# Index scores in pieces of 512 keys instead of 1024, with four places of scores and six of relu

## What is computed

```
logits = einsum('bqhd,bsd->bqhs', qib, ki)
iscore = einsum('bqhs,bqh->bqs', relu(logits), wib)
iscore = where(allowed, iscore, -inf)
_, idx = top_k(iscore, 256)
```

## Time and profile before

| | us |
|---|---|
| median of three runs | 3299.3 |
| the profiled execution's own time | 3305.6 |
| its span | 3303.9 |
| PE busy in the span | 3102.3 (94%) |
| DVE busy in the span | 1741.4 (53%) |
| ACT busy in the span | 1551.2 (47%) |
| index stretch, half 0 (DVE's first sum to the first search instruction) | 304.4 to 438.7 |
| index stretch, half 1 | 653.8 to 810.2 |

### The profile page before, as it was taken

The page is one execution under the profiler, slowest core; times in us unless marked ns, Lnnn a source line. Parts: engine busy times, 40 slices in busy tenths (PEclk is TensorE's granted clock), DMA queues, the critical chain, the costliest instruction groups (busy, mean ns, idle before and its releaser), DMA issues. The chain is left out here.

```text
span 3303.9 us, 43020 instructions
## 1 busy us (share of the span) xinstructions
PE 3102.3 (94%) x15772; PEld 2522.9 (76%) x15772; DVE 1741.4 (53%) x3657; ACT 1551.2 (47%) x2448; POOL 957.6 (29%) x701
## 2 busy tenths in 40 slices
PE   7995999899996999998999799979999999989998
PEld 6994888777884667776778678868888888878787
DVE  6774799989996566547531166642211231133423
ACT  4544689766992667772111133324444354431111
POOL 3441012200221556652222233312222222222222
PEclk9996999999997999999999899989999999999999
DMA  5656333253334521116552344464344533355522
GB/s 173 204 184 224 99 109 101 81 185 114 102 96 155 191 89 41 52 50 183 142 140 102 140 144 151 142 220 136 118 128 141 195 122 122 120 158 153 135 102 89
DMA packets 431706, 440.63 MB, mean 133 GB/s; under 512 B 31008, under 2 KB 324256, under 8 KB 431392
## 3 DMA queue, kind: packets, MB, share of 16 engines
q1 hardware_dynamic: 431520, 438.18, 43.1%
HBM read 279.51 MB, written 158.60 MB: 133 GB/s over the span
## 5 line engine op out<-in xcount | busy, mean ns | idle before, releaser
L1403 PE MATMUL p_pr<-p_hT,p_w_hi 128*128 128x512 f32 x896 | 354.8, 396 | 15.6 <-POOL p_w_lo L1156 10.3
L1404 PE MATMUL p_pr<-p_hT,p_w_hi 128*128 128x512 f32 x896 | 352.3, 393 | 0.0
L1405 PE MATMUL p_pr<-p_hT,p_w_lo 128*128 128x512 f32 x896 | 351.8, 393 | 0.0
L1684 POOL TENSOR_TENSOR a_prob<-a_prob,a_inv 128x1024 f32<-128x1024 f32 (+12 forms) x104 | 250.7, 2419 | 211.6 <-DVE a_inv L1729 211.4
L1196 ACT ACTIVATE p_relu<-p_isc,p_level 128x2048 int8<-128x2048 f32 (+5 forms) x192 | 276.5, 1442 | 22.6 <-DVE p_level L1293 17.7
L1156 POOL TENSOR_TENSOR p_w_lo<-p_w_raw,p_w_hi 128x256 fp32r<-128x256 f32 x144 | 107.5, 779 | 604.9 <-DVE p_level L1293 401.6
L844 PE MATMUL t_pj_ps<-t_w_hi,t_hT_slot 128*128 128x356 f32 (+2 forms) x768 | 269.6, 351 | 13.5 <-DVE t_w_lo L692 7.4
L1704 DVE CUSTOM_DVE_ANT_0 a_prob<-a_s_ps,a1n_mask 128x512 f32<-128x512 f32 (+3 forms) x320 | 189.4, 608 | 141.5 <-PE a_s_ps L1838 136.9
L846 PE MATMUL t_pj_ps<-t_w_hi,t_hT_slot 128*128 128x356 f32 (+2 forms) x768 | 263.2, 343 | 0.0
L845 PE MATMUL t_pj_ps<-t_w_lo,t_hT_slot 128*128 128x356 f32 (+2 forms) x768 | 262.7, 342 | 0.0
L2749 PE MATMUL t2n_pr<-t2n_hT,t2n_w_hi 128*128 128x512 f32 x584 | 231.8, 397 | 0.0
(11 more groups left out here) (291 smaller groups left out, 7122.9 us busy)
## 6 DMA issues: line engine op xcount, KB each, us to landing
s_hT<-t_hT_slot SPq DMA_DIRECT2D x32, 1024.0 KB, 6.0
s_gT<-p_o_sb SPq DMA_DIRECT2D x128, 256.0 KB, 4.9
o_gates<-s_gT SPq DMA_DIRECT2D x64, 512.0 KB, 5.0
p_w_raw<-in_w_in SPq DMA_DIRECT2D x56, 512.0 KB, 4.3
t2n_w_raw<-in_w_in SPq DMA_DIRECT2D x56, 512.0 KB, 4.2
s_qT<-t_qT_slot SPq DMA_DIRECT2D x32, 512.0 KB, 2.7
p_hT<-s_hT SPq DMA_DIRECT2D x32, 512.0 KB, 9.8
s_zuT<-p_o_sb SPq DMA_DIRECT2D x64, 256.0 KB, 4.9
```

What stands on the lines that cost most here:

```text
L1403: nc.tensor.matmul(pr[n % NPR][:], wh, hi, start=(k == 0), stop=False)
L1404: nc.tensor.matmul(pr[n % NPR][:], wh, lo, start=False, stop=False)
L1405: last = nc.tensor.matmul(pr[n % NPR][:], wl, hi, start=False, stop=(k == KD - 1))
L1684: nc.gpsimd.tensor_tensor(p, p, f, ALU.mult).then_inc(normed, 1)
```

## The change

A piece holds 512 keys (`BANK`) instead of 1024. `sc_ps` has 4 places and `relu` 6 slots, each half as wide. A half has 152 entries instead of 88 and the same 152 score matmuls. `FROM[0]` goes from entry 16 to 28, and `SPLIT_AT` from 5, 8, 11 to 9, 14, 19. Mask steps keep their entry numbers.

```diff
--- before.py
+++ after.py
@@ -917,7 +917,7 @@
 BATCHES = [((15, 11, 5), (13, 9, 7, 3)), ((14, 10, 4), (12, 8, 6, 2))]
 NB = 7
 NACT = 3
-KEYS = 1024
+KEYS = BANK
 
 
 def phase_first(c, stack):
@@ -932,7 +932,7 @@
         [(p, 0) for p in range(CHUNKS - LEAD, CHUNKS)] + [(p, 1) for p in range(CHUNKS - LEAD, CHUNKS)]
     N_HALF = len(PLACES)
     N_UNITS = 2 * N_HALF
-    SLOTS_W, NPR, NO, NRELU = 3, 4, 4, 3
+    SLOTS_W, NPR, NO, NRELU, NSC = 3, 4, 4, 6, 4
     TRIES = 32
     TRY_OF = [30 - j for j in range(31)]
 
@@ -961,8 +961,8 @@
     N_HEADS = len(HEADS[0])
     IDX_UNITS = [(0, 15), (52, 72)]
     TRY_UNITS = [(15, 52), (72, 106)]
-    FROM = [16, 0]
-    SPLIT_AT = [5, 8, 11]
+    FROM = [28, 0]
+    SPLIT_AT = [9, 14, 19]
 
     def first_head(half, b):
         return min(x for x, head in enumerate(HEADS[half]) if head[0] == b)
@@ -1022,7 +1022,7 @@
     room = sb("room", [P, NB], F32)
     halfway = sb("halfway", [P, 1], F32)
     pr = [ps(f"pr{n}", [P, BANK]) for n in range(NPR)]
-    sc_ps = [ps(f"sc_ps{n}", [P, KEYS]) for n in range(2)]
+    sc_ps = [ps(f"sc_ps{n}", [P, KEYS]) for n in range(NSC)]
 
     h_loaded = [[sem(f"h_loaded{g}{k}") for k in range(KD)] for g in range(UNITS)]
     w_loaded = [sem("w_even"), sem("w_odd")]
@@ -1186,7 +1186,7 @@
                 act.wait_ge(scored, e + 1)
                 if e >= NRELU:
                     act.wait_ge(summed, e - NRELU + 1)
-                nc.scalar.activation(relu[:, e % NRELU, 0:n], sc_ps[e % 2][:, 0:n], ACT.Relu).then_inc(relued, 1)
+                nc.scalar.activation(relu[:, e % NRELU, 0:n], sc_ps[e % NSC][:, 0:n], ACT.Relu).then_inc(relued, 1)
 
             def count(half, j):
                 act.wait_ge(cand_ready, half * TRIES + j + 1)
@@ -1413,11 +1413,11 @@
                     pe.wait_ge(ki_loaded, 16)
                 if k0 == 0 and h == 0:
                     pe.wait_ge(qi_loaded[q % 2], 16 * (q // 2 + 1))
-                if e >= 2:
-                    pe.wait_ge(relued, e - 1)
+                if e >= NSC:
+                    pe.wait_ge(relued, e - NSC + 1)
                 for j in range(0, n, BANK):
                     w = min(BANK, n - j)
-                    last = nc.tensor.matmul(sc_ps[e % 2][:, j:j + w], qiT[:, q % 2, h, :], kiT[:, k0 + j:k0 + j + w],
+                    last = nc.tensor.matmul(sc_ps[e % NSC][:, j:j + w], qiT[:, q % 2, h, :], kiT[:, k0 + j:k0 + j + w],
                                             start=True, stop=True)
                 last.then_inc(scored, 1)
```

## The result

The changed kernel takes 3313.7 us (median of 6 runs, 3312.8 to 3317.6) against 3299.0 for the kernel before (6 runs): a ratio of 1.0042, 95% interval 1.0032 to 1.0052. It is slower by 14.7 us; 3312 was forecast. The profiled execution took 3317.6 us.

A forecast was written before the change was run, and what follows sets the result against it. DVE's index work and, with ACT's counts, its search were taken as the bound. Half 0 +2.0 and half 1 +10.6, search and tail 0, sum to +12.6: 3299.3 becomes 3312 us, range 3302 to 3328.

The forecast's parts named there:

- DVE's index work and the search stages as the bound: Phase: DVE with ACT's counts sets search length; the change is worth what it moves DVE's index ends, 438.65 and 810.15.
- The price of a further instruction: DVE's chained index sums: 0.32 us per further sum, 0.37 per head-0 product, taken as 20.5 us a half.
- Half 0: First index stretch: -0.85 + 20.5 - (21.6 - 4.0) = +2.0 us, bounds -0.5 to +8.
- small misses: Half 0: 1.9 us of DVE waits, added to 2.1 for the weight chunk to give 4 us of waits left.
- Half 1: Second index stretch: -0.4 + 20.5 - (13.0 - 3.5) = +10.6 us, bounds +8.6 to +20.
- I take 3.5 us of waits left: Half 1: of DVE's 13.0 us of waits 3.5 stay, at the first sum and the second group of activations.
- Nearly all of it comes from an uneven mix: DVE's index waits: 256-key entries get as much projection work as 1024-key ones, starving DVE of relu in narrow pieces.
- The signs: Profile signs of being right: 512-key sums x196, starts 0.85 us apart, DVE 95% busy in half 0, search stages unchanged.
- Tail: After the search: DVE's 5.8 us wait for a mask store and attention's loads shift rigidly, change 0.
- B: Index halves: waits are only cut up by more round trips; half 0 +8, half 1 +20, 3327 us; chance 0.19.
- C: Later stages: search waits and the mask-store wait give time back, +12.6 becomes +3.8, 3303 us; chance 0.15.
- D: DVE's short sums don't show their drain and cost 0.06 us further each, so the even spread wins: 3291 us; chance 0.08.

The follow-up runs named there:

- the chained split: Against the kernel before, only DVE sums entries of more than 512 keys in two instructions, the second waiting for the first: 3314.6 us, ratio 1.0050.

## Why the prediction was right, point by point

- **DVE's index work and the search stages as the bound.** Right. Search 0 and search 1 kept 202.8 and 180.0 us to 0.1, and the shift of the last mark before them went through.
- **The price of a further instruction.** 20.5 us a half were forecast. In half 0 the stretch grew by 1.8 us while waits fell by 19.6: 21.4 us, 0.33 each. In half 1 it grew by 13.8 while waits fell by 4.1: 17.9, 0.28 each. The split on DVE alone reproduced a loss of this size, at 0.24 to 0.27 each. The runs show what the price consists of: chained, 512 columns start 0.85 us apart, unchained 0.66, and the columns are 0.54 of either. So 0.12 us is the instruction's own, and 0.19 us is the wait for the sum just before. The Trainium skill (Perfetto Trace Analysis, Optimizing Scalar/DVE Operations) gives about 60 ns, by which the 128 instructions would be an estimated 8 us of DVE's time; the measurement decides, and here even the unchained sum costs twice that.
- **Half 0.** +2.0 forecast against +0.7. The waits left were 2.0, not 4.0; the term of 1.9 for "small misses" was too high. The price was 0.9 higher than forecast and took some of that back. The first product came at 325.7 instead of 327.
- **Half 1.** +10.6 forecast against +13.8. The term that was too small is "I take 3.5 us of waits left": 8.9 were left. About 4 of the 5.4 more are there because ACT stood behind `mask_keep` in a stream whose entries had become shorter: with the sign pass later 4.9 are left. What the rest is stays open. I had looked at the mask steps as a burst for PE and DVE, and not at who is in line behind ACT's sign pass. The price, 2.6 us below the forecast for the half, hid half of this.
- **The reason given for the waits.** "Nearly all of it comes from an uneven mix" was wrong. The spread by width left them where they were, in half 1 too (12.7 us where it was 13.0). The sum still held, because in half 0 what counts is DVE's work against PE's time and both had been worked out.
- **Luck.** The forecast had 1.3 us too much in half 0 and 3.2 too little in half 1, and put the tail (-1.2) and the rest of the span (-1.4) at nothing. So the profiled execution grew by 12.0 us where 12.6 were forecast; that is closer than the terms are.
- **The signs.** The pitch of 0.85, the count of 196 and the search stages came as said. DVE was to be busy 95% of half 0 and was 89% (121.1 of 136.0 us). It hardly waited for relu, but the time between chained sums is too short to be listed as a wait and isn't busy either. PE's new waits for relu in half 1 were not short: 17.7 us in six, the longest 4.9, where it was 7.9 in six.
- **Tail.** Taken as rigid. It gave back 1.2 us: the wait for the mask store went from 5.8 to 4.6. The waits view of DVE, and PE's first attention scores:

```profile
DVE p_mask L1351 <- DMA s_mask<-p_mask: 4.6, 1, 4.6
...
1063.71 1.51 PE L1838 MATMUL a_s_ps<-a1n_kT,a1n_qT 128*128 128x128 f32 x6 [16.80 <-PEq L2882]
```

- **Rivals.** B (waits stay) did not come, but with the old number of places the same pieces land at 3327.9, B's 3327, with 11.1 and 15.3 us of waits where B had 10 and 13. C did not come; the search kept its waits. D's condition, sums that don't show their drain (the wait for the sum before), is met only when the loop order is changed, and then half 0 binds on PE, as D said. Even so such a sum costs 0.12 us and not D's 0.06, and D's 3291 is not reached.

## What to carry to other kernels

Before a piece is made smaller, look at the engine that accumulates: if each accumulation waits for the one just before it, each further instruction costs that wait as well as its own overhead (about 0.3 us together here), and idle time of that engine hides it only where another engine sets the stretch. If pieces must be small, put the loop that changes the accumulator's columns inside. Whatever is placed by entry number (sign passes, mask steps, splits) moves in time when entries shrink, and what stands in line behind it on its engine should be looked up one by one.

## What was not expected of the hardware

- A chained and an unchained sum of the same 512 columns both last 0.75 us in the records, but start 0.85 and 0.66 us apart: 0.19 us of difference that no duration shows. With a wait for the sum before alone, inside an entry of the chained split, it is 0.78.
- Four waits of ACT for DVE's mask, 18.9 us together, cost DVE about 4 us, and the time nothing that these runs can tell.
- Behind the phase of the change, where all kernels run the same instructions, the rest of the span varied from 2247.1 to 2253.9 us between profiles. So differences below some 5 us are read here from stretches, not from totals. The three profiles with a rest near 2247 us have the highest granted clocks of the whole span, 0.971 and 0.972, and the others 0.967 to 0.970. That the clock makes the difference was not tested. DVE's first sum also starts anywhere from 301.4 to 304.4 us, so half 0 is read by its length as well as by its end.
